# Bias tables laid out in device memory during the first stage, and a strip's values in one transfer

## What is computed

```python
h = rms_norm(x, norm_gain) * (1 + scale) + shift
qa, ka, va, ga, qr, kr, vr, gr = split(h @ w_in)            # 8 parts of 512
# attention, 8 heads of 64: a query row r sees 8 key rows from start = clip(r - 4, 0, rows - 8),
# a block of 16 query columns sees 32 key columns, of which 16 are valid
s = einsum('bhnqd,bhrnkd->bhnqrk', q_b, k_blk) + bias[head, row offset, column offset]   # -inf where not valid
o = softmax(s) @ v_blk
na = o * silu(ga)
ret = rms_norm(retention(qr, kr, vr)) * silu(gr)
y = x + gate * (concat(na, ret) @ w_out)
```

## Time and profile before

| | |
|---|---|
| median of 3 runs | 3742.84 us (3740.99 to 3746.05) |
| span of the profiled execution | 3741.3 us, 51265 instructions |
| TensorE busy | 3615.6 us, 97% |
| VectorE, ScalarE, GpSimd busy | 1512.5, 883.6, 500.3 us |
| granted TensorE clock, mean | 0.853 |
| moved by DMA | 477.72 MB, mean 128 GB/s |

### The profile page before, as it was taken

The page is one execution under the profiler, slowest core; times in us unless marked ns, Lnnn a source line. Parts: engine busy times, 40 slices in busy tenths (PEclk is TensorE's granted clock), DMA queues, the critical chain, the costliest instruction groups (busy, mean ns, idle before and its releaser), DMA issues. The chain is left out here.

```text
span 3741.3 us, 51265 instructions
## 1 busy us (share of the span) xinstructions
PE 3615.6 (97%) x17152; PEld 3096.3 (83%) x17152; DVE 1512.5 (40%) x3183; ACT 883.6 (24%) x1832; POOL 500.3 (13%) x462
## 2 busy tenths in 40 slices
PE   5999999999999999999999699999999999799999
PEld 1888888888778888888888589999999999688887
DVE  3333333333443333333333243333333334577775
ACT  2222222222321111111111143333333333111111
POOL 0111111111100000000000021111111111233332
PEclk8999999999999999999999875555555555799999
DMA  7344444444522222222222394336564431556564
GB/s 271 128 149 149 150 149 150 152 147 146 196 74 76 84 76 86 75 84 77 76 81 78 98 223 104 70 88 145 129 137 117 93 85 22 181 198 207 201 208 147
DMA packets 230406, 477.72 MB, mean 128 GB/s; under 512 B 30152, under 2 KB 104648, under 8 KB 227658
## 3 DMA queue, kind: packets, MB, share of 16 engines
q1 hardware_dynamic: 229196, 472.83, 41.6%
q0 software_dynamic: 1152, 4.19, 0.3%
HBM read 305.46 MB, written 171.47 MB: 127 GB/s over the span
## 5 line engine op out<-in xcount | busy, mean ns | idle before, releaser
L287 PE MATMUL proj<-w_att_hi,a_h_hi 128*128 128x512 f32 x2560 | 1025.1, 400 | 15.9 <-DVE w_att_lo L263 8.2
L287 PE MATMUL proj<-w_att_hi,a_h_lo 128*128 128x512 f32 x2560 | 1001.6, 391 | 0.0
L287 PE MATMUL proj<-w_att_lo,a_h_hi 128*128 128x512 f32 x2560 | 999.8, 391 | 0.0
L287 PEld LDWEIGHTS proj<-w_att_hi,a_h_hi 128*128 128x128 f32 x2560 | 483.0, 189 | 109.0 <-DVE w_att_lo L263 9.5
L287 PEld LDWEIGHTS proj<-w_att_hi,a_h_lo 128*128 128x128 f32 x2560 | 481.7, 188 | 103.5
L1255 PEld LDWEIGHTS o_bank<-v_strip,probs_T 120*128 120x128 f32 x2560 | 561.6, 321 | 0.0
L287 PEld LDWEIGHTS proj<-w_att_lo,a_h_hi 128*128 128x128 f32 x2560 | 483.4, 189 | 92.4
L1255 PE MATMUL o_bank<-v_strip,probs_T 120*128 120x64 f32 x2560 | 556.0, 396 | 0.0
L1233 PE MATMUL s_bank<-k_strip,q_block 128*128 128x480 f32 x640 | 353.9, 653 | 38.4 <-DMA bias_tables<-bias_rows 33.7
L1176 DVE COPY probs_T<-t_bank 120x512 f32<-120x512 f32 x160 | 110.7, 692 | 674.5 <-PE t_bank L1242 674.5
L1137 ACT ACTIVATE probs<-biased,neg_max 128x480 f32<-128x480 f32 x320 | 221.2, 691 | 548.9 <-DVE neg_max L1168 548.9
(11 more groups left out here) (131 smaller groups left out, 3452.6 us busy)
## 6 DMA issues: line engine op xcount, KB each, us to landing
k_strip<-kT_d SPq DMA_DIRECT2D x20, 1920.0 KB, 11.1
a_x<-in_x SPq DMA_DIRECT2D x40, 512.0 KB, 4.6
a_xT<-in_xT SPq DMA_DIRECT2D x40, 512.0 KB, 5.3
h_d<-a_h_hi SPq DMA_DIRECT2D x40, 512.0 KB, 2.7
h_d<-a_h_lo SPq DMA_DIRECT2D x40, 512.0 KB, 3.5
vg_d<-vg SPq DMA_DIRECT2D x40, 512.0 KB, 3.0
kT_d<-k_parts SPq DMA_DIRECT2D x80, 256.0 KB, 4.6
q_strip<-qT_d SPq DMA_DIRECT2D x40, 512.0 KB, 7.0
```

What stands on the lines that cost most here:

```text
L287: last = self.nc.tensor.matmul(bank, h[:, par, k, :], w[:, k, cols], start=(k == 0 and j == 0), stop=(k == KB - 1 and j == 2))
```

## The change

The masked and filled tables are built in device memory, `tables_d`, for the three kinds of strip and all 8 heads, while the first in-projection runs: after pairs 1, 2 and 3 SyncE issues three transfers of 1920 KB each of a constant (`mask_table`), and from pair 5 to pair 16 two transfers of 384 KB from `bias_rows` into `tables_d` per pair (`place_bias`). The attention stage then fetches a filling in one transfer of 2880 KB (the first in three of 960 KB, by kind), with no memset, no mask copy and no pieces. Values are stored by the in-projection in the order of a strip (`v_d`, four transfers of 64 KB per tile) and fetched in one transfer of 960 KB per strip; the gate is stored apart (`ng_d`). SyncE's loop over the pairs is written out. TensorE's wait for the first bias goes, VectorE's stays.

```diff
+EDGES = ("top", "inner", "bottom")
+
+
+def window_of(edge, r):
+
+    if edge == "top":
+        key0, dr0 = max(r - 4, 0), max(r - 4, 0) - r + WIN_H - 1
+    elif edge == "inner":
+        key0, dr0 = r, 3
+    else:
+        key0, dr0 = min(r - 4, 0) + KR - QR, min(r - 4, 0) - r + WIN_H - 1
+    return key0, dr0
...
             def store_vg(t, par):
                 wait_apart(sp, vg_made, 2 * t + 2)
-                sp.dma_start(vg_d[t], vg[:, par, :]).then_inc(vg_stored[par], 16)
+                for g in range(2):
+                    for r in range(2):
+                        sp.dma_start(v_d[g, 2 * t + r].rearrange("w c n -> c w n"),
+                                     vg[r * W:(r + 1) * W, par, g * GW:(g + 1) * GW]).then_inc(vg_stored[par], 16)
+                sp.dma_start(ng_d[t], vg[:, par, HALF:D]).then_inc(vg_stored[par], 16)
+
+            def mask_table(e):
+
+                for kind in range(3):
+                    sp.dma_start(tables_d[e, :, kind], masked[:].unsqueeze(1).to_broadcast([P, NH, KEYS])
+                                 ).then_inc(masked_placed[e], 16)
+
+            def place_bias(e, r):
+
+                key0, dr0 = window_of(EDGES[e], r)
+                rows = bias_rows.rearrange("c k hr x -> c (k hr x)").rearrange("c (kh rx) -> c kh rx", kh=3 * NH)
+                table = tables_d[e].rearrange("p k h x -> p (k h) x")
+                sp.dma_start(table[r * QC:(r + 1) * QC, :, key0 * KC:(key0 + WIN_H) * KC],
+                             rows[:, :, dr0 * KC:(dr0 + WIN_H) * KC]).then_inc(tables_made, 16)
...
-            over_pairs(sp, body)
+            for i in range(PAIRS):
+                body(i, i == PAIRS - 1)
+                if i == 1:
+                    sp.wait_ge(masked_made, 1)
+                if 1 <= i <= 3:
+                    mask_table(i - 1)
+                if i == 5:
+                    for e in range(3):
+                        sp.wait_ge(masked_placed[e], 48)
+                if 5 <= i <= 16:
+                    for n in range(2 * (i - 5), 2 * (i - 4)):
+                        place_bias(n // QR, n % QR)
             for par in range(2):
                 wait_apart(sp, f.h_stored[par], 32 * PAIRS)
-                wait_apart(sp, vg_stored[par], 16 * PAIRS)
+                wait_apart(sp, vg_stored[par], 80 * PAIRS)
             wait_apart(sp, qk_stored, 96 * PAIRS)
+            sp.wait_ge(tables_made, 16 * 3 * QR)
...
             def load_v(b, half):
                 g, q0, k0 = rows_of(b, half)
                 wait_apart(sp, valued, STEPS * b + HALF_STEPS * (half - 1))
-                for r in range(KR):
-                    sp.dma_start(v_strip[r * 8:(r + 1) * 8, half],
-                                 vg_rows[k0 + r, :, g * GW:(g + 1) * GW].rearrange("(c w) n -> w c n", w=8)
-                                 ).then_inc(v_in[half], 16)
+                sp.dma_start(v_strip[0:GROUP_KEYS, half].rearrange("p c n -> p (c n)"),
+                             v_d[g, bass.ds(k0, KR)].rearrange("r w c n -> (r w) (c n)")).then_inc(v_in[half], 16)
...
-            def fill(n, kinds=range(3)):
-
-                g, edge = FILLS[n]
-                landed = first_in if n == 0 and kinds[0] == 0 else tables_in[n]
-                for r in range(QR):
-                    if edge == "top":
-                        key0, dr0 = max(r - 4, 0), max(r - 4, 0) - r + WIN_H - 1
-                    elif edge == "inner":
-                        key0, dr0 = r, 3
-                    else:
-                        key0, dr0 = min(r - 4, 0) + KR - QR, min(r - 4, 0) - r + WIN_H - 1
-                    for k in kinds:
-                        rows = bias_rows[:, k].rearrange("c (h r) x -> c h (r x)", h=NH)
-                        sp.dma_start(tables[r * QC:(r + 1) * QC, n % 2, k, :, key0 * KC:(key0 + WIN_H) * KC],
-                                     rows[:, g * GH:(g + 1) * GH, dr0 * KC:(dr0 + WIN_H) * KC]
-                                     ).then_inc(landed, 16)
+            def fill(n):
+
+                g, e = FILLS[n]
+                sp.dma_start(tables[:, n % 2], tables_d[e, :, :, g * GH:(g + 1) * GH]).then_inc(tables_in[n], 16)
+
+            def fill_first():
+
+                g, e = FILLS[0]
+                for kind, landed in enumerate((first_in, tables_in[0], tables_in[0])):
+                    sp.dma_start(tables[:, 0, kind], tables_d[e, :, kind, g * GH:(g + 1) * GH]).then_inc(landed, 16)
 
             def refill(n, b):
 
                 wait_apart(sp, biased_made, STEPS * (b + 1))
-                sp.dma_start(tables[:, n % 2], masked_d).then_inc(masked_placed, 16)
-                wait_apart(sp, masked_placed, 16 * n)
                 fill(n)
...
             load_qk(0, 0)
+            fill_first()
             load_v(0, 0)
-            wait_apart(sp, cleared[0], 1)
-            fill(0, [0])
-            wait_apart(sp, cleared[0], 3)
-            fill(0, [1, 2])
             load_qk(0, 1)
             load_v(0, 1)
-
-            wait_apart(sp, cleared[1], 1)
-            sp.dma_start(masked_d, tables[:, 1]).then_inc(masked_placed, 16)
-            wait_apart(sp, masked_placed, 16)
             fill(1)
...
-            for k in range(3):
-                nc.vector.memset(tables[:, 0, k], MASKED).then_inc(cleared[0], 1)
             for g in range(NH // GH):
                 b0, n0 = g * G_BODIES, 3 * g
                 if g == 0:
-                    dve.wait_ge(first_in, 16 * QR)
+                    dve.wait_ge(first_in, 16)
                 else:
-                    dve.wait_ge(tables_in[n0], 48 * QR)
...
 
-            pe.wait_ge(first_in, 16 * QR)
             for j in range(4):
                 score(0, j)
...
-        vg_d = dram("vg_d", (TILES, P, D))
+        v_d = dram("v_d", (NH // GH, T // W, 8, W // 8, GW))
+        ng_d = dram("ng_d", (TILES, P, HALF))
         na_d = dram("na_d", (TILES, P, HALF))
         h_d = dram("h_d", (TILES, 2, P, D))
-        masked_d = dram("masked_d", (P, 3, GH, KEYS))
+        tables_d = dram("tables_d", (len(EDGES), P, 3, NH, KEYS))
         part_d, qf_d, kv_d, rg_d = (dram(n, (TILES, P, HALF)) for n in ("part_d", "qf_d", "kv_d", "rg_d"))
```

More of the change, by code:

```diff
@@ L401, in attention_in_stage @@
         vg = sb("vg", [P, 2, D])
+        masked = sb("masked", [P, KEYS])
         turned = sb("qkT", [P, 2, 4, 2 * P])
@@ L412, in attention_in_stage @@
         vg_stored, qk_stored = [sem("vg_stored0"), sem("vg_stored1")], sem("qk_stored")
+        masked_made, masked_placed = sem("masked_made"), [sem(f"masked_placed{e}") for e in range(3)]
+        tables_made = sem("tables_made")
         block = ctx.enter_context(nc.Block())
@@ L462, in _ @@
             nc.gpsimd.memset(f.ones[:], 1.0).then_inc(f.ones_made, 1)
+            nc.gpsimd.memset(masked[:], MASKED).then_inc(masked_made, 1)
             f.rstd_x(pool, 0)
@@ L952, in _, with attention_stage @@
             outputs(s, 1)
-def attention_stage(nc, qT_d, kT_d, vg_d, bias_rows, ident, masked_d, w_out, na_d):
+def attention_stage(nc, qT_d, kT_d, v_d, tables_d, ident, w_out, na_d):
     with ExitStack() as ctx:
@@ L993, in attention_stage @@
         GROUP_KEYS = KR * 8
-        FILLS = [(g, edge) for g in range(NH // GH) for edge in ("top", "inner", "bottom")]
+        FILLS = [(g, e) for g in range(NH // GH) for e in range(len(EDGES))]
         @block.sync
@@ L1115, in _ @@
             place_q(0, 1)
-            nc.gpsimd.memset(tables[:, 1], MASKED).then_inc(cleared[1], 1)
             for u in range(2, UNITS):
@@ L1193, in body @@
                     if first and k == GH:
-                        dve.wait_ge(tables_in[0], 32 * QR)
+                        dve.wait_ge(tables_in[0], 32)
                     if k % 2 == 1 and not (first and k < 2):
@@ L1207, in _ @@
                 if g == 0:
-                    dve.wait_ge(first_in, 16 * QR)
+                    dve.wait_ge(first_in, 16)
                 else:
-                    dve.wait_ge(tables_in[n0], 48 * QR)
+                    dve.wait_ge(tables_in[n0], 16)
                 body(b0, n0 % 2, g == 0)
-                dve.wait_ge(tables_in[n0 + 1], 48 * QR)
+                dve.wait_ge(tables_in[n0 + 1], 16)
                 with dve.Fori(b0 + 1, b0 + G_BODIES - 1) as b:
                     body(b, (n0 + 1) % 2)
-                dve.wait_ge(tables_in[n0 + 2], 48 * QR)
+                dve.wait_ge(tables_in[n0 + 2], 16)
                 body(b0 + G_BODIES - 1, n0 % 2, last=g > 0)
@@ L1250, in value @@
                     if u % COLS == 0:
-                        pe.wait_ge(v_in[u // COLS], 16 * KR * (b + 1))
+                        pe.wait_ge(v_in[u // COLS], 16 * (b + 1))
                     at_least(pe, scaled, UNITS * b + u - 1)
```

17 lines of the change are left out of this document (8 added, 9 removed).

## The result

The changed kernel takes 3791.86 us (median of 4 runs, 3789.01 to 3795.77), the kernel before beside it 3742.53 us: ratio 1.0129, 95% interval 1.0114 to 1.0144. The forecast was 3774 us, 0.9% slower, in a range of 3755 to 3810: right side and range, with 49 us measured for 31 forecast. The page of the kernel after, beside the earlier trace rows: the same picture, except that the granted clock of slice 24, where the attention steps begin, is 0.5 where it was 0.7.

What follows compares the result with a forecast made beforehand. TensorE, busy at 90% or more nearly everywhere, bounds the kernel by its pauses and its clock. Attention +26.0, stores +2 and tables +5 make 33 us on the 3741.3 us span: 3774 us, 0.9% slower, range 3755 to 3810.

Steps and rivals of the forecast that it cites:

- Attention stage: Attention start: first value group 12.4 us earlier, but 28 steps at half clock instead of full; net +26.0 us.
- the two holes forecast: Attention start: TensorE waits for the first table, then for values until 2147.5 us, so it enters the mix at half clock.
- The second pause: Second body of the attention stage: TensorE's 4.7 us wait goes, already counted in the +26.0 us.
- Stores: First in-projection: four more transfers per tile on SyncE delay later loads and a weight block; +2 us.
- Tables in the first in-projection: After pairs 1, 2 and 3, three 1920 KB transfers ahead of the x load stall TensorE 1.8 us a pair; +5 us.
- the wait ahead of the norm's spread: First in-projection: TensorE waits 0 to 3 us before the matmul spreading the norm, in each of three pairs.
- The 24 device-to-device transfers: First in-projection: two 384 KB transfers a pair take 6.5 us, inside 14 us of cover; nothing.
- Rival 1: Attention stage starts at full clock and keeps it, its pause gone: 3265 us, chance 0.07; full for one body: 0.02.
- Rival 2: Attention stage: unbroken work alone brings the clock back early and no pause ends it; 3265 us, chance 0.03.
- Rival 3: First in-projection: table transfers at the slow store rate, TensorE waiting some 16 us in three pairs; 3820 us, chance 0.10.
- my likeliest case: Whole kernel: half clock from the attention start, tables cheap; 3763 to 3793 us, chance 0.72.

Runs made afterwards that it cites:

- the order with the separate wait: Changed kernel with the first table ahead of q, k and values, two tables behind, and a semaphore for the last table: 3289.50 us; masks also spread: 3269.18 us.
- the run where it was put in: Kernel with new start order, separate wait and spread masks, but q and k of the second body fetched after 30 scored steps, not 16: 3733.39 us.
- the value part alone: Kernel before with only values stored strip by strip and fetched in one 960 KB transfer; bias tables as before: 3731.46 us, ratio 0.9973.
- the two profiles with a burst: Kernel before, and the same with the change's value part, each with step four's score matmuls of the second body issued 12 times: 3550.50 and 3441.17 us.
- table part alone: Changed kernel with values, their stores and fifteen 64 KB transfers a strip as in the kernel before: 3794.25 us, ratio 1.0142.
- with the masks spread: Changed kernel with one mask transfer after each of pairs 1 to 9: 3771.43 us; with new start order and separate wait too: 3269.18 us.
- the best kernel: Changed kernel with masks spread over nine pairs, new load order at the attention start and a separate wait for the last table: 3269.18 us, ratio 0.8730.
- the changed kernel with the burst: Changed kernel with the two score matmuls of step 20 of the first body issued 12 times over: 3324.35 us, ratio 0.8885.
- all three runs that entered it at half: Score matmuls of one step issued 12 times in the changed kernel (3324.35 us), the kernel before (3550.50) and the changed kernel with old value handling (3326.78).

## Why the forecast was right, and where it was short

- **Attention stage, forecast +26.0, measured +25.1 with the output stage.** The mechanism is the one forecast. From the end of the last retention matmul to the end of the last value group it is +26.1, and the output stage gives 1.0 back. That both sums say 26 is partly luck, since two misses of the same size cancel. The first value group came 11.1 us sooner, counted from the last retention matmul, where 12.4 was forecast, 1.3 us lost; and from there to the end of the last value group 1068.0 us passed instead of 1030.8, 37.2 more where 26.0 + 12.4 = 38.4 was forecast, 1.2 us won. Of the two holes forecast ahead of it the first was only 0.23 us, and the clock did rise for 3.4 us; the second was 7.34 us, twice what was forecast, and in it the clock fell. The steady mix entered at 0.50 and stayed there, against full clock for 28 steps in the kernel before. That the holes decide this is shown by the order with the separate wait: same transfers, no hole, full clock. (A slip of reading ahead of this: the page's row has the clock at half in ten slices, not eleven.)
- **The second pause goes: right, and worth nothing here**, since the clock was at half already. At full clock one such pause of 8.00 us cost 464 us, in the run where it was put in.
- **Stores, forecast +2, measured +3.0** in the value part alone, over both in-projection stages (+1.6 between the two profiles with a burst, which have the same code there). Of the 3.0, 0.8 are idle time and 1.7 a stretch of 3.4 us more at half clock around the change of weights.
- **Tables in the first in-projection, forecast +5: the term that failed.** With tables and stores together the two stages grew by 21.0, of which 3.0 are the stores alone; 14.2 are the tables alone (table part alone: 2045.94 against 2031.71), and 3.8 come only when both are there.

  What I had priced, the wait ahead of the norm's spread, was sized about right in this profile: xT landed 18.2 us later than in the kernel before (issued 192.10, landing after 5.3; here 204.72 and 12.7, less the 1.8 us by which the work around it is shifted) where 15.5 + 2.0 = 17.5 was forecast, and the three waits are 1.88, 2.92 and 1.18 us, where I had 1.8 each. In three other profiles of the same code they sum to 7.9 to 9.9 us instead of 6.0, and the two kinds of wait together to 13.2 to 14.0.

  Two things were missing. First, the stall is not one per pair but two, 13.1 us in six: I had followed x to the norm's diagonal and its spread, and not on to the second tile's `a_h_lo`, which TensorE waits for 1.44, 2.87 and 2.84 us. The late spread costs more than its own lateness there: VectorE takes it up 5.1 us after it is done (220.63 to 225.75 us), behind its work for q and k, where in the kernel before it does so after 0.1 us (193.47 to 193.60).

  Second, the stalls cost clock as well, for which the forecast had no term: the records have it at half for 3.4 us, three times, 10.2 us in which half the work is done, 5.1 us more. A fourth such stretch, 1039.3 to 1042.7 us, around the change of weights, where the kernel before has two and this one three, is 1.7 more. 13.1 + 5.1 + 1.7 is 19.9 of the 21.0.
- **The 24 device-to-device transfers, forecast nothing: right**, 650.00 busy us of 650.00 from 350 to 1000 us, at clock 1.00.
- **Rival 1, full clock kept, 3265 us.** It didn't occur in the kernel as changed, but it was near: three lines of order and one wait away (3269 us with the masks spread, 3289.5 without). My price for the stage was right, 320 steps of 1.777 are 568.6 us, against 1075.2; that 3289.5 lies 24 us over my 3265 is mostly the tables' term again. **Rival 2**, that work alone brings the clock back, is refuted for this mix by a further 1055 busy us of 1055 at half clock. **Rival 3**, 16 us of stall a pair, didn't occur either: the measured stall is 3.3 to 5.8 us a pair.

The total lies 18 us above my 3774 and still in the range, in part by luck: my likeliest case ended at 3793 with 34.3 us for the attention stage, which took 26.1, and 2 + 15 for the first stages, which took 21.0, so the margin of the one covered the miss in the other.

What stays open: 1.1 of the 21.0 us in the first stages have no row, less than the scatter between profiles. And by what the chip decides on a short hole isn't settled, its length alone doesn't say: TensorE lost the clock in one of 2.94 and one of 2.91 us, kept it in one of 2.62 us and in one of 2.92 us between projections (272.41), and lost it there around one of 1.88 us.

## What to carry to other kernels

Look at the granted clock before anything else: where TensorE is busy in every microsecond and the clock is at half, find the hole in which it fell, and whether the work behind it has ever brought it back; here a hole of 8 us cost 464 us, more than every transfer removed could give, and holes of 2.81 to 7.34 us lost the clock too, though one of 2.62 didn't. Follow a late load past the first instruction that waits for it, to everything made from it. Order the loads at a stage's start so that the first steps run without a hole (only the first table ahead of q, k and values, the others behind), and let each wait ask only for what its step reads. Bulk transfers that are put into a busy stage go one at a time between the loads that the stage needs.

## What the runs showed of the hardware

- The attention mix held either clock for as long as it ran: 1067 us at 0.50 with the masks spread, 568 us at 1.00 in the best kernel, at 100% and 99.8% busy, through all six table fetches.
- The projections recover from a fall by themselves in 3.4 us (220.09 to 223.50 us), and in 6.8 in two other profiles (323.2 to 330.0 us in the changed kernel with the burst, 285.4 to 292.2 in the table part alone); the attention mix doesn't in 1067 us. In a row of 24 score matmuls of 480 columns without a gap the clock rose in all three runs that entered it at half, 3.1 to 5.1 us after its start, and stayed until the next hole or the stage's end.
- At full clock the limits are others than at half: with the old filling, strips that were on time at 3.360 us a step were 2.9 to 5.0 us late at 1.777.
